# Three key units of each layer issued by GpSimd's DMA queue instead of SyncE's

## The reference

```
h = rmsnorm(x); z = h @ w_in                       # 1024 columns into all branches and gates
A: latent attention; q_lat = q_nope @ w_uk          # sample group against a paged cache:
   s_past = q_lat @ ckv_past + q_rope @ kr_past     #   8 sequences x 32 pages x 128 positions
   pr = softmax(scale * [s_past, s_new]); o = pr @ [ckv_past, ckv_new] @ w_uv
B: chunked spatial gating (128 positions, 8 groups);  C: gated linear attention (4 heads)
x = x + (sum of gated branches) @ w_o;  x = x + swiglu(rmsnorm(x))
```

## Time and profile before

| | us |
|---|---|
| median of 3 runs | 2017.96 |
| lowest, highest | 2010.59, 2018.74 |
| profiled execution, whole | 2016.56 |
| its span in the trace | 2014.9 |
| PE busy in the span | 1986.1 |
| DVE, ACT, POOL busy | 1010.6, 712.8, 273.9 |
| mean granted TensorE clock, share of full | 0.989 |

### The profile page before, as it was taken

The page is one execution under the profiler, slowest core; times in us unless marked ns, Lnnn a source line. Parts: engine busy times, 40 slices in busy tenths (PEclk is TensorE's granted clock), DMA queues, the critical chain, the costliest instruction groups (busy, mean ns, idle before and its releaser), DMA issues.

```text
span 2014.9 us, 48295 instructions
## 1 busy us (share of the span) xinstructions
PE 1986.1 (99%) x20222; PEld 1898.0 (94%) x20222; DVE 1010.6 (50%) x1575; ACT 712.8 (35%) x1141; POOL 273.9 (14%) x520
## 2 busy tenths in 40 slices
PE   9999999999999999999999999999999999999998
PEld 9989988889999999999999899887999999999998
DVE  7765422376656444433367653324675554444333
ACT  5464122365333222222235631413642332222221
POOL 0004555400000000000000055563000000000000
PEclk9999999989999999999999999999999999999999
DMA  6428999932433333323353399998224332333232
GB/s 226 162 75 272 339 344 360 332 98 67 129 103 95 88 93 93 95 87 90 97 183 129 110 298 344 326 369 293 81 62 136 105 95 85 94 95 95 87 94 73
DMA packets 140976, 322.34 MB, mean 160 GB/s; under 512 B 24420, under 2 KB 72087, under 8 KB 140247
## 3 DMA queue, kind: packets, MB, share of 16 engines
q10 hardware_dynamic: 46944, 147.87, 23.9%
q1 hardware_dynamic: 69238, 100.05, 14.5%
q0 software_dynamic: 24576, 71.34, 10.1%
HBM read 307.08 MB, written 12.08 MB: 158 GB/s over the span
## 4 chain that ended last, share of the span: by engine, by line
PE 93%; DVE 2%; DMA 2%; ACT 1%; SPq 1%; issue 1%; ACTq 0%; DVEq 0%
PE PS L1957 27%; PE PS L1959 26%; PE PS L1958 26%; PE PS L2234 3%; PE PS L2262 3%; PE PS L2010 2%; DMA kp<-in_cache_keys 1%; SPq L2623 1%; PE PS L2125 0%; PE PS L2289 0%; PE PS L2390 0%; PE PS L2428 0%; PE PS L1996 0%; DMA xT<-in_x_t 0%; PE PS L2017 0%
## 5 line engine op out<-in xcount | busy, mean ns | idle before, releaser
L1957 PE MATMUL PS<-hh,wh 128*128 128x260 f32 x3008 | 864.7, 287 | 2.2 <-issue 1.0
L1959 PE MATMUL PS<-hl,wh 128*128 128x260 f32 x3008 | 855.2, 284 | 0.0
L1958 PE MATMUL PS<-hh,wl 128*128 128x260 f32 x3008 | 854.6, 284 | 0.0
L1957 PEld LDWEIGHTS PS<-hh,wh 128*128 128x128 f32 x3008 | 572.2, 190 | 16.8 <-issue 14.4
L1959 PEld LDWEIGHTS PS<-hl,wh 128*128 128x128 f32 x3008 | 572.4, 190 | 0.0
L1958 PEld LDWEIGHTS PS<-hh,wl 128*128 128x128 f32 x3008 | 571.7, 190 | 0.3
L725 DVE TENSOR_TENSOR wl<-raw,wh 128x1024 fp32r<-128x1024 f32 (+4 forms) x326 | 351.3, 1079 | 306.0 <-ACT wh L1481 305.2
L1481 ACT ACTIVATE wh<-raw 128x1024 fp32r<-128x1024 f32 (+4 forms) x326 | 304.7, 937 | 528.8 <-PE PS L1959 521.3
L1957 PE MATMUL PS<-fh,wh 128*128 128x260 f32 x704 | 199.5, 283 | 0.0
L1959 PE MATMUL PS<-fl,wh 128*128 128x260 f32 x704 | 198.9, 282 | 0.0
L1958 PE MATMUL PS<-fh,wl 128*128 128x260 f32 x704 | 198.8, 282 | 0.0
(11 more groups left out here) (363 smaller groups left out, 2808.6 us busy)
## 6 DMA issues: line engine op xcount, KB each, us to landing
raw<-in_wpack ACTq DMA_DIRECT2D x238, 512.0 KB, 3.6
kp<-in_cache_keys POOLq DMA_DIRECT2D x256, 144.0 KB, 4.4
kp<-in_cache_keys SPq DMA_DIRECT2D x256, 144.0 KB, 4.6
vpg<-in_cache_vals SPq DMA_DIRECT2D x256, 128.0 KB, 4.8
vpg<-in_cache_vals POOLq DMA_DIRECT2D x256, 128.0 KB, 4.9
raw<-in_wpack ACTq DMA_DIRECT2D x48, 256.0 KB, 3.4
raw<-in_wpack ACTq DMA_DIRECT2D x16, 384.0 KB, 3.2
x_keep<-xT SPq DMA_DIRECT2D x2, 2080.0 KB, 9.7
```

The lines of the kernel that those rows point to most:

```text
L1957: pe.matmul(out, w[0], x[0], start=first, stop=False)
L1958: pe.matmul(out, w[1], x[0], start=False, stop=False)
L1959: return pe.matmul(out, w[0], x[1], start=False, stop=last)
```

## The change

Two lists are made, and the two loops run over them. `KEYS_BY_POOL` is the odd units from 3 on and 12, 20 and 28, in the order in which they are read: 3, 5, 7, 9, 11, 12, 13, 15, 17, 19, 20, 21, 23, 25, 27, 28, 29, 31. `KEYS_BY_SP` is 2, 6, 0, 4, 10, 8, 14, 16, 18, 22, 24, 26, 30. With unit 1 GpSimd issues 19 units a layer (16 before), SyncE 13 (16 before). Slots, waits, pages and the work of TensorE stay.

```diff
+KEYS_BY_POOL = [w for w in KEY_ORDER if (w % 2 and w > 1) or w in (12, 20, 28)]
+KEYS_BY_SP = [2, 6, 0, 4, 10, 8] + [w for w in KEY_ORDER if w > 10 and w % 2 == 0 and w not in KEYS_BY_POOL]
@@ SyncE
-                for i in range(16):
-                    w = (2, 6, 0, 4, 10, 8)[i] if i < 6 else 2 * i
+                for i, w in enumerate(KEYS_BY_SP):
                     numbers = page_numbers(mybir.EngineType.SP, w)
@@ GpSimd
-                for w in range(3, 32, 2):
+                for w in KEYS_BY_POOL:
                     numbers = page_numbers(mybir.EngineType.Pool, w)
                     if KEY_HOLDER[w] is not None:
                         pool.wait_ge(*upto(f"read K{KEY_HOLDER[w]}"))
```

## The result

| | before | after |
|---|---|---|
| median of 6 runs each, us | 2014.28 | 2029.49 |
| lowest to highest | 2010.17 to 2020.55 | 2024.72 to 2033.77 |
| profiled execution, its span | 2014.9 | 2029.2 |
| ratio of times | | 1.0073, 95% interval 1.0054 to 1.0092 |

The changed kernel is slower by 0.73%, some 15 us, where 3 us of gain were forecast and 2021 us was the upper end. The profiled spans differ by 14.3 us.

What follows compares the result with a forecast made beforehand. TensorE, busy 99% of 2014.9 us, bounds the kernel; key stalls are 4.9 us. -4.9 + 0.7 + 0.7 + 0.5 = -3.0 us gives 2013.6 profiled, 2015.0 median; range 2007 to 2021 us.

Steps and rivals of the forecast that it cites:

- Gain on the even steps: Key steps b10 and b12: unit 22 issued earlier ends b10's 0.87 us; 26 lands at 264.4 and 1262.8.
- b12: Key step reading units 24 and 26: no stall forecast in layer 0, 0.5 us in layer 1.
- cost nothing: Moving units 12 and 28 to GpSimd's queue: its idle time (5.79, 6.79 us) absorbs them, later units stay in time.
- the last transfers of a unit on SP's queue take 10.0 to 13.4 us to land: SP's queue before b12: transfers of one queue are served late; GpSimd's take 6.7 and 7.0 us.
- Unit 28 ... cost nothing: GpSimd's queue between 27 and 29: unit 28 fills 6.79 us of idleness; 29 starts no later than now.
- b11: Key step that wants unit 23, issued 2.9 and 2.8 us later: new stalls of 0.7 us in each layer.
- the 7 us of GpSimd's last transfer of 23: GpSimd's queue before b11: 23's last transfer takes 7.0 and 6.7 us, landing at 258.3 and 1254.6.
- b10's wait: Key step reading units 20 and 22: its 0.87 us stall in layer 1 goes, as SP issues 22 earlier.
- Unit 31 and the values behind: End of GpSimd's key list: 31 lands at 284.6, 3 us in time for b15; values start no later.
- C: Rival, chance 0.15: GpSimd's queue becomes the late one at b11; stalls of 12.4 us, sum +7.5, 2024.1 us.
- B: Rival, chance 0.15: bytes decide, stalls only move to other steps; 0 +-1 us, 2016.6.
- The rule of taking queues in turn by packets: DMA engines: GpSimd's packets, about three times as large, favour its units; b11's stall under 0.7 us, sum near -4.9.

Runs made afterwards that it cites:

- alternating lists: From unit 9 on, one unit of each key step on each queue, against the kernel before: ratio 0.9956; the same with queues exchanged: 0.9966.
- the longer rows: The changed kernel with SP's transfers from unit 12 on reading 64 rows of 2304 bytes, not 128 of 1152: ratio 0.9994 to the kernel before.

## Why the prediction was wrong

**The step that failed** is "Gain on the even steps": "the last transfer of 26 should take what that of 22 took: 10.0 us in layer 0, 11.0 us in layer 1". It took 17.40 and 16.71 us, and so b12, put at 0 and 0.5 us, waited 8.14 and 7.09 us. I had looked at the state of SP's own queue, and that was as I said: unit 22 had landed at 244.93, just before 24's first issue at 245.25. But how fast a unit on it lands depends on the other queue too. When 20 and 22 were served in the kernel before, GpSimd paused for 3.38 us; in the changed kernel, from 230.27 to 269, it never paused for more than a microsecond.

**The pauses were counted as free.** "GpSimd computes nothing in this stage either" is right, and the starts of 20, 21, 23 and 28 came within 0.5 us of the forecast. But the pauses were time in which SP's queue got more of the engines. The longest shows how much: from 264 to 273 us, in and after the pause of 6.79 us, SP's queue moved 2.06 MB before (first row) and 0.96 MB after (second), and it had units under way all that time in both.

```profile
q1 hardware_dynamic: 2013, 2.06, 70.4%
```

```profile
q1 hardware_dynamic: 938, 0.96, 33.9%
```

These rows show what a pause is worth, not what made 26 late: before, 26 had landed at 267.82, early in this stretch. For 26 the pauses ahead of 21 and 25 count, and those unit 20 fills; unit 20 alone made b12 wait 4.25 and 2.25 us. The idle time that "cost nothing" relied on was looked at only for the delays of GpSimd's own units, not for SP's.

**A reading that was too wide.** That "the last transfers of a unit on SP's queue take 10.0 to 13.4 us to land" is true of units 22 and 26, from which it was read; those of 20, 24, 28 and 30 took 6.8 to 8.2 us in the same profile. So not every unit was slow on SP's queue, and a unit right ahead of it may count as well as the other queue. In the changed kernel unit 22 had none right ahead and GpSimd did not pause, and its last transfer took 9.21 and 10.34 us; 26, behind 24, took 17.40 and 16.71 us. How much each of the two adds is not separated. Likewise the 23 transfers "in a row" of layer 1 have a pause of 5.3 us in them: 22's last was issued at 1236.29 and 24's first at 1241.55, when its slot fell free.

**"Unit 28 ... cost nothing"** was right for 28 alone and wrong in the sum: in the changed kernel b12 waits 3.2 and 2.4 us less when 28 is held back.

**b11** was right in place and size (0.7 forecast; 0.58 and 1.02 us), as were the 7 us of GpSimd's last transfer of 23 (6.5 and 6.6 us). So was the end of b10's wait, as far as one profile tells. Unit 31 and the values behind made no wait.

**The clock** was not in the sum at all: each wait of 7 or 8 us is paid again by half clock behind it, 1.75 and 2.32 us. The longest wait in the profile I worked from, 2.96 us, had none behind it.

**The rivals.** C had the sign and half of the size (+7.5 us of some 15) but the wrong queue and step: it let GpSimd's queue become late at b11, where it never took more than 6.6 us, and the late one was SP's at b12. B, the bytes, is refuted by the alternating lists, which need the same bytes in less time. The rule of taking queues in turn by packets (the Trainium skill, "DMA: Bandwidth & Descriptors", Queues, rings and completion order) I had weighed with the wrong half of its consequence: what it gives GpSimd's queue it takes from SP's. By that rule 26 had to lose, and the trace and the longer rows agree with it as to the direction. A strict one for one, counted in the profile's packets, they don't show: from 259 to 269 us it was 676 of GpSimd's to 909 of SP's. I used the row of unequal packets to lower a stall and did not ask what stood on the other queue.

## What to carry to other kernels

In this kernel, with the DMA engines full, a transfer's time depended on what the other queue held: before moving work to a queue that pauses, ask which transfer of the other queue lands in that pause. Balance the queues within each deadline, not over the stage: one of the two units of every step on each queue did what no moving of single units did. The shortest way to see it is the bytes of each queue in the stretch before the stall, beside the total.

## What was not expected of the hardware

Of two 144 KB transfers issued within 0.2 us of each other, the one on GpSimd's queue landed after 7.6 us and the one on SP's after 14.4 us. In the profiles of before, after and the two alternating lists, the last transfers of units 20 to 28 took 3.9 to 7.6 us on GpSimd's queue and 6.8 to 17.4 us on SP's.

Half clock came behind every wait for keys from 3.57 us up (3.57, 4.25, 4.26, 4.35, 4.38, 4.71, 4.95, 4.98, 7.09, 8.14 and 8.29 us; where the row has all 64 matmuls of the step together they took 3.10 to 3.64 us instead of 1.95). Below that it went either way: it came behind waits of 2.90, 2.69, 2.65, 2.48 and 2.25 us, and not behind 2.96, 2.38, 2.02 and 2.00 us.

Two profiles of the kernel before have nearly the same sum of waits (4.9 and 5.6 us) on different steps (b12, b10). A single profile does not give the place, and its sum is that of one execution.
